# Expert weights on two DMA queues: down projections loaded through ScalarE's queue, gate and up projections through SyncE's

## What is computed

```python
def expert_choice_moe(h, w_router, b_router, w_gate_e, w_up_e, w_down_e):
    ...
    cap = EC_CAPACITY * s // N_EXPERTS
    ...
    vals, idx = lax.top_k(jnp.swapaxes(probs, 1, 2), cap)
    xe = jax.vmap(lambda hb, ib: hb[ib])(h, idx)
    a = jnp.einsum('becd,edf->becf', xe, w_gate_e)
    u = jnp.einsum('becd,edf->becf', xe, w_up_e)
    y = jnp.einsum('becf,efd->becd', jax.nn.silu(a) * u, w_down_e)
    y = y * vals[..., None].astype(y.dtype)
    ...
```

## Time and profile before

| | |
|---|---|
| runs (3) | 1414.45, 1414.14, 1411.67 us; median 1414.14 |
| profiled execution | 1413.32 us, its span 1411.2 us |
| TensorE busy | 77% of the span |
| VectorE, ScalarE, GpSimd busy | 23%, 17%, 6% |
| read from HBM | 494.71 MB |
| mean granted clock of TensorE | 0.858 of full speed |

### The profile page before, as it was taken

The page is one execution under the profiler, slowest core; times in us unless marked ns, Lnnn a source line. Parts: engine busy times, 40 slices in busy tenths (PEclk is TensorE's granted clock), DMA queues, the critical chain, the costliest instruction groups (busy, mean ns, idle before and its releaser), DMA issues.

```text
span 1411.2 us, 16312 instructions
## 1 busy us (share of the span) xinstructions
PE 1080.0 (77%) x7073; PEld 610.5 (43%) x7073; DVE 323.1 (23%) x462; ACT 246.4 (17%) x355; POOL 87.6 (6%) x95
## 2 busy tenths in 40 slices
PE   4899999896767677565776757757677677996888
PEld 1779999632212122121231213212132133996777
DVE  1546347410000000000000000000000003665455
ACT  1423533200000000000000000000000004643634
POOL 2000000000000000000000000000000002421122
PEclk9899999698887878898677896897778888998989
DMA  9997786699999999999999999999999998742321
GB/s 331 381 340 259 245 301 259 249 400 430 428 426 428 430 427 429 429 427 429 428 428 429 429 428 429 429 427 429 429 427 429 429 427 307 267 129 85 116 66 55
DMA packets 89013, 496.38 MB, mean 352 GB/s; under 512 B 5080, under 2 KB 57724, under 8 KB 61068
## 3 DMA queue, kind: packets, MB, share of 16 engines
q1 hardware_dynamic: 87296, 490.36, 85.7%
q0 software_dynamic: 1296, 5.19, 1.1%
q10 hardware_dynamic: 380, 0.23, 0.1%
HBM read 494.71 MB, written 1.05 MB: 351 GB/s over the span
## 4 chain that ended last, share of the span: by engine, by line
DMA 58%; PE 32%; DVE 4%; ACT 3%; issue 1%; SPq 0%; POOL 0%; DVEq 0%; ACTq 0%
DMA ring<-in_w_down_e 20%; DMA ring<-in_w_up_e 18%; DMA ring<-in_w_gate_e 18%; PE psum L603 7%; PE psum L604 6%; PE psum L605 6%; PE psum L878 4%; PE psum L904 2%; DMA ring<-in_w_in 2%; PE psum L671 1%; ACT ring_r L1097 1%; PE psum L855 1%; ACT arena L1229 1%; PE psum L1019 1%; PE psum L911 1%
## 5 line engine op out<-in xcount | busy, mean ns | idle before, releaser
L878 PE MATMUL psum<-ring,arena 128*32 128x512 f32 x2048 | 301.7, 729 | 131.4 <-DMA ring<-in_w_gate_e 76.3
L904 PE MATMUL psum<-ring,arena 128*32 128x512 f32 x992 | 171.2, 820 | 105.4 <-DMA ring<-in_w_down_e 99.4
L878 PEld LDWEIGHTS psum<-ring,arena 128*32 128x32 f32 x2048 | 64.3, 125 | 344.2 <-issue 144.0
L904 PEld LDWEIGHTS psum<-ring,arena 128*32 128x32 f32 x992 | 35.1, 130 | 224.8 <-DMA ring<-in_w_down_e 168.7
L603 PE MATMUL psum<-ring_r,ht_hi 128*128 128x256 f32 (+1 forms) x384 | 115.3, 300 | 10.2 <-DVE ht_lo L1353 7.2
L1349 DVE TENSOR_TENSOR ring_r<-ring,ring_r 128x2048 fp32r<-128x2048 f32 x43 | 101.9, 2393 | 70.6 <-ACT ring_r L1097 70.5
L603 PE MATMUL psum<-ht_hi,ring_r 128*128 128x256 f32 x384 | 109.3, 285 | 6.0 <-issue 6.0
L605 PE MATMUL psum<-ring_r,ht_lo 128*128 128x256 f32 (+1 forms) x384 | 113.5, 295 | 0.0
L604 PE MATMUL psum<-ring_r,ht_hi 128*128 128x256 f32 (+1 forms) x384 | 113.2, 295 | 0.0
L1097 ACT ACTIVATE ring_r<-ring 128x2048 fp32r<-128x2048 f32 x55 | 103.1, 1907 | 45.2 <-DMA ring<-in_w_in 28.0
L605 PE MATMUL psum<-ht_hi,ring_r 128*128 128x256 f32 x384 | 108.2, 282 | 0.0
(11 more groups left out here) (260 smaller groups left out, 965.5 us busy)
## 6 DMA issues: line engine op xcount, KB each, us to landing
ring<-in_w_gate_e SPq DMA_DIRECT2D x64, 2048.0 KB, 35.5
ring<-in_w_up_e SPq DMA_DIRECT2D x64, 2048.0 KB, 35.8
ring<-in_w_down_e SPq DMA_DIRECT2D x62, 2048.0 KB, 35.9
ring<-in_w_in SPq DMA_DIRECT2D x38, 1024.0 KB, 8.6
ring<-in_w_ada SPq DMA_DIRECT2D x24, 1024.0 KB, 11.0
ring<-in_w_conv_out SPq DMA_DIRECT2D x4, 1024.0 KB, 5.9
ring<-in_w_o SPq DMA_DIRECT2D x4, 1024.0 KB, 11.3
extra<-in_w_down_e SPq DMA_DIRECT2D x2, 2048.0 KB, 11.9
```

The source lines that it names most:

```text
L878: last = mm(psum[32 * g:32 * g + 32, b, :], cur[h][:, k, :], w[:, g, :], start=(k == 0), stop=(k == KD - 1), tile_position=(0, 32 * g))
L904: last = mm(psum[32 * q:32 * q + 32, 2 + n, :], act_t[:, f % 4, (f // 4) * CAP:(f // 4 + 1) * CAP], w[:, kk, n * BANK:(n + 1) * BANK], sta ...
```

## The change

The helper `load_pair` gets the issuing engine as an argument and stands ahead of the engines' programs. SP now issues the whole first expert, and of all others gate and up only. ACT issues the down pairs of all other experts, 4 for each of 15 experts, in its own program: ahead of an expert's sigmoid stand the four waits and loads of that expert's down projection. Sizes, places, semaphores and what each load waits for stay as they were. The first two experts are taken out of ACT's loop, since the first has no loads there.

```diff
+        def load_pair(eng, i, e):
...
+            eng.dma_start(shaped(to.rearrange("p a b -> p (a b)"), k=k, n=src.shape[2]), src).then_inc(loaded[at], 16)
...
             for e in range(2 * (PAIRS + EXTRA), 2 * EXPERT_SLOTS, 2):
-                sp.wait_ge(slot_used, HEAD_SLOTS + released(e))
-                load_pair(0, e)
+                if e < EXPERT_SLOTS or e % EXPERT_SLOTS < 16:
+                    sp.wait_ge(slot_used, HEAD_SLOTS + released(e))
+                    load_pair(sp, 0, e)
             with sp.Fori(1, NE // 2) as i:
                 for e in range(2 * EXPERT_SLOTS, 4 * EXPERT_SLOTS, 2):
-                    sp.wait_ge(slot_used, 2 * EXPERT_SLOTS * i + (HEAD_SLOTS - 2 * EXPERT_SLOTS + released(e)))
-                    load_pair(i, e)
+                    if e % EXPERT_SLOTS < 16:
+                        sp.wait_ge(slot_used, 2 * EXPERT_SLOTS * i + (HEAD_SLOTS - 2 * EXPERT_SLOTS + released(e)))
+                        load_pair(sp, i, e)
...
-            with act.Fori(0, NE // 2) as i:
+            def expert(i, h):
+
+                act.wait_ge(slot_used, 2 * EXPERT_SLOTS * i + (HEAD_SLOTS + h * EXPERT_SLOTS + 8))
+                f(sig_a, bank(0), ACT.Sigmoid).then_inc(sig_ready, 1)
...
+            def load_down(i, h):
+
+                for j in range(16, EXPERT_SLOTS, 2):
+                    e = 2 * EXPERT_SLOTS + h * EXPERT_SLOTS + j
+                    act.wait_ge(slot_used, 2 * EXPERT_SLOTS * i + (HEAD_SLOTS - 2 * EXPERT_SLOTS + released(e)))
+                    load_pair(act, i, e)
+
+            expert(0, 0)
+            for e in range(EXPERT_SLOTS + 16, 2 * EXPERT_SLOTS, 2):
+                act.wait_ge(slot_used, HEAD_SLOTS + released(e))
+                load_pair(act, 0, e)
+            expert(0, 1)
+            with act.Fori(1, NE // 2) as i:
                 for h in range(2):
...
+                    load_down(i, h)
+                    expert(i, h)
```

More of the change, by code:

```diff
@@ L464, in build @@
         szt = shaped(room(7), k=KD, s=SEQ)
+        def load_pair(eng, i, e):
+            h, j = divmod(e % (2 * EXPERT_SLOTS), EXPERT_SLOTS)
+            w = t[("w_gate_e", "w_up_e", "w_down_e")[j // 8]][0]
+            w = w[bass.ds(2 * i + h, 1)]
+            rows, k = (2 * P, 2) if j < 16 else (4 * P, 4)
+            first = (j % 8) // 2 * rows
+            src = w[:, first:first + rows, :].rearrange("e (p k) n -> p (e k) n", k=k)
+            at = expert_place(e)
+            to = extra[:, at - RING:at - RING + 2, :] if at >= RING else ring[:, at:at + 2, :]
+            eng.dma_start(shaped(to.rearrange("p a b -> p (a b)"), k=k, n=src.shape[2]), src).then_inc(loaded[at], 16)
         block = ctx.enter_context(nc.Block())
@@ L478, in _ @@
                 sp.dma_start(slot_in(s, k=src.shape[1], n=src.shape[2]), src).then_inc(loaded[place(s)], 16)
[L480 to L490, removed]
             def load_first(d):
-                load_pair(0, 2 * d)
+                load_pair(sp, 0, 2 * d)
             for d in range(4):
@@ L1203, in _ @@
             f(lam_s[:, 2:4], lam_s[:, 0:2], ACT.Exp).then_inc(lam_exps, 1)
-            with act.Fori(0, NE // 2) as i:
-                for h in range(2):
[L1207 to L1212, removed]
+            def expert(i, h):
+                act.wait_ge(slot_used, 2 * EXPERT_SLOTS * i + (HEAD_SLOTS + h * EXPERT_SLOTS + 8))
+                f(sig_a, bank(0), ACT.Sigmoid).then_inc(sig_ready, 1)
+                act.wait_ge(gw_turned, 2 * i + (h + 1))
+                f(gwt, bank(3, t=4, m=P)[:, 0:TT, :], ACT.Copy).then_inc(gwt_ready, 1)
+                act.wait_ge(act_turned, 2 * i + (h + 1))
+                f(act_t, bank(0, c=4, m=P), ACT.Copy).then_inc(act_t_ready, 1)
+            def load_down(i, h):
[9 more added lines that the diff above has]
+            with act.Fori(1, NE // 2) as i:
+                for h in range(2):
+                    load_down(i, h)
+                    expert(i, h)
             split_ahead([first_slot["q_diff"], first_slot["q_diff"] + 1])
```

## The result

The changed kernel is slower: 1425.79 us (median of 4 runs, 1424.09 to 1428.37) against 1413.97 of before, a ratio of 1.0091 with a 95% interval of 1.0078 to 1.0103. The forecast was 1423, with 1415 to 1433 as the range. The profiled execution took 1424.09 us, its span 1421.9, 10.7 more than before.

What follows compares the result with a forecast made beforehand. The experts were taken to last as long as their bytes need, plus TensorE's work behind the last byte. All terms were 0 except the end's +9.4 us: 1413.3 + 9.4 = 1422.7, stated as 1423, range 1415 to 1433.

Steps and rivals of the forecast that it cites:

- Issue time: 60 load instructions move from SP to ACT, hidden behind waits and other work: cost 0.
- bytes and rate: Same bytes through the same 16 engines, already busy without gaps, so a second queue gains 0.
- the middle: Experts 1 to 14: downs often land before ups, but the bytes in flight don't suffer: cost 0.
- Case C: Rival: landed downs hold places, fewer loads are in flight, 20 us lost over 14 experts, end 1443; chance 0.10.
- Order of landing: Two queues share the engines equally, so a down pair need no longer land behind its expert's up pairs.
- case B: Rival, not slower: SP's queue gets much more than half, last expert's downs still land behind ups; 1413 to 1414; chance 0.15.
- The end: Last expert: behind the last up's landing come an up pair, 2.43 us and four down pairs: +9.4 us, ends +3.7 and +16.7.
- x: Time from the last up pair's landing to the experts' last byte: 0 to 4.9 us, taken as 2.45.
- the prediction's two cases: Last expert: downs through after 8 pairs' time, or PE late and SP with some 4 pairs left when ACT starts its four.
- The tail: After the experts: its first load, issued some 5 us before the end, is in time; the tail moves as a whole: 0.
- The rule: Skill page: loads of all issuing engines interleave, several issuers save only sequencer time; by it the change is worth nothing, 1413.3.

Runs made afterwards that it cites:

- e1: Changed kernel with the last expert's four down pairs back on SP's queue, the other 56 staying on ACT: 1414.39 us, ratio 1.0005.
- e2: Kernel before the change, with only the last expert's four down pairs on ACT's queue: 1428.88 us, ratio 1.0106.
- e8: Kernel before the change, all loads on SP's one queue, the last expert's four down pairs issued ahead of its up pairs: 1429.60 us, ratio 1.0116.
- e10: The changed kernel itself, run once more with nothing altered: 1424.43 us, ratio 1.0075 against the kernel before.
- e5: Kernel before the change, with the tail's first four loads held back until all but one of the last expert's slots are used: 1417.82 us, ratio 1.0028.
- e3: Kernel with up and down pairs of all experts but the first on ACT's queue, gate pairs on SP's: 1415.20 us, ratio 1.0010 against before.

## Why the prediction was right

**Issue time, bytes and rate, the middle: 0 each.** Right. The rate from 500 to 700 us was 429 GB/s for 428, and e1, with 56 pairs on ACT, is 1.0005 of before. Case C, a new gap, didn't come: the share of the engines from 500 to 700 us is still 1.01.

**Order of landing.** Equal shares were read from two small loads of other engines beside SP's; the up pairs 9.8 us apart and 2.15 against 2.13 MB in 10 us show them for two queues of 2 MB loads. That rules out case B, which needed 4 to 1.

**The end.** The mechanism is shown three times: e1 and e2 place all of it in the last expert's four down loads, and e8 makes it with one queue. Its terms: the last byte was to stay at 1179.2 and came at 1180.0; x was set at 2.45 and was 3.6 (of the prediction's two cases the second came: SP's four ups were all still to land when ACT issued its first down at 1140.7); the up pair was set at 2.57 and took 3.64; the way to the first down 2.43, and it took 2.41; the four downs 10.3, and they took 7.10. The sum was +9.4 and became +7.1. The up pair was slow and the downs fast for the same reason, the clock: 0.50 was granted from 1176.5 to 1180 us and 1.00 from 1182.5 to 1189.5, and one mean of 2.57 for both didn't tell them apart. In e10 the clock from 1182.5 to 1189.5 was 0.77 and the downs took 8.55; in e2 they took 8.79. Both are nearer to the 10.3.

**The tail.** "So the tail moves as a whole: 0" is the step that failed. It was worth 2.4 us (11.9 for 9.5). The step compared when the first load would land with when TensorE needs it. It looked at the first load alone, and had it issued some 5 us before the end (it was 3.3 us, at 1186.22; before, it was 11). It left out the second, issued at 1187.85 and landed 7.9 us later, whose conversion the chain goes through. And it left out that these two conversions stand on ACT, and VectorE's half of the first on VectorE, ahead of the work that the tail's first product waits for. e5 prices a somewhat longer wait without the change at 3.7 us.

So 9.4 was forecast for the end alone, and 7.1 + 2.4 = 9.5 came from the end and the tail: the close hit of the number owes something to luck, to two errors that cancel. From the tail's first product to the end of the span it is 1.3 us more (220.4 for 219.2), which was not looked into. The medians are 11.8 us apart where these two profiled executions are 10.7; the changed kernel's profiled one was the fastest of its four, with the shortest burst of downs of any profile.

**The rule** that was weighed, the Trainium skill, DMA: Bandwidth & Descriptors, "Issuing engines are not separate DMA queues", holds in its first half: loads of both engines interleave, and the rate is the same. That issuing from several engines only saves issue time is not so here: it changed which load lands first, and the time went up by 11.8 us. The same page, "Queues, rings and completion order", says that an engine takes packets in turn from the queue rows that have work; the 9.8 us between up pairs and the even split of the bytes agree with it.

## What to carry to other kernels

In a stage bound by its loads, look at what is still to be computed when the last byte lands: the last load should be the one with the least work behind it. In these runs a second DMA queue brought no bandwidth to engines that were full, but it gave up the order in which data is needed; if loads are spread over queues, keep those of one chain on one queue, as e3 does. And where a stage ends, ask what the next one's first loads wait for, and which engine has their conversion in its program ahead of work that is due.

## What the runs showed of the hardware

With both queues full, the pairs of one came every 9.8 us and the total stayed at 428 to 429 GB/s (1150 to 1170 us), so sharing was equal to within what the trace resolves. Each of the last three up pairs of the changed kernel's last expert followed a wait of 3.5 to 6.3 us and took 3.51 to 3.64 us, with a granted clock of 0.50 to 0.53, the lower level of 1.2 GHz. In the uninterrupted burst of four downs a pair took 7.10/4 = 1.78, with a granted clock of 1.00, the level of 2.4 GHz, in the stretch that holds it:

```profile
1182.00:1190.00 8.00, 7.10 (x64) 2.27 (x64) 0.34 (x1) 0.24 (x1) 0.00 (x0) 1.00 0.29 77
```

The same burst took 7.10 to 9.67 us in four profiles of kernels with this order, which may be part of why their times spread more than those of before; single profiles don't show how much.
